# Tile 2's heads in tile 3's order, and its causal mask added once by VectorE to the decay columns

## What is computed

```python
def forgetting_attention(q, k, v, log_f):
    c = jnp.cumsum(log_f, axis=-1)
    for i in range(S // Q_BLOCK):                 # tiles of 128 queries
        q0, q1 = i * Q_BLOCK, (i + 1) * Q_BLOCK
        logits = jnp.einsum('bhqd,bhkd->bhqk', qf[:, :, q0:q1], kf[:, :, :q1])
        logits = logits + c[:, :, q0:q1, None] - c[:, :, None, :q1]
        logits = jnp.where(s_pos <= t_pos, logits, -jnp.inf)
        p = jax.nn.softmax(logits, axis=-1)
        outs.append(jnp.einsum('bhqk,bhkd->bhqd', p, vf[:, :, :q1]))
...
        mixed = jnp.concatenate([attn, pool], axis=-1)
        x = x + jnp.einsum('bse,ed->bsd', mixed, w_out[layer])
```

## Time and profile before

| | us |
|---|---|
| median of 3 runs | 2385.66 (2385.27 to 2389.16) |
| span of the profiled execution | 2541.9 |
| TensorE matmuls busy in it | 2151.2 (85%) |
| VectorE busy | 1499.3 (59%) |
| GpSimd busy | 1020.5 (40%) |
| ScalarE busy | 653.7 (26%) |
| mean granted TensorE clock | 0.898 |
| HBM traffic, mean | 330 GB/s |

### The profile page before, as it was taken

The page is one execution under the profiler, slowest core; times in us unless marked ns, Lnnn a source line. Parts: engine busy times, 40 slices in busy tenths (PEclk is TensorE's granted clock), DMA queues, the critical chain, the costliest instruction groups (busy, mean ns, idle before and its releaser), DMA issues.

```text
span 2541.9 us, 29123 instructions
## 1 busy us (share of the span) xinstructions
PE 2151.2 (85%) x10694; PEld 1516.7 (60%) x10694; DVE 1499.3 (59%) x3505; ACT 653.7 (26%) x1838; POOL 1020.5 (40%) x1028
## 2 busy tenths in 40 slices
PE   8999998999999986996675366276879799999998
PEld 7999785666666975874431254221366555545695
DVE  3441179999999368647454677710067665886321
ACT  6772235566555121001010101110122000001220
POOL 0000014555665113435566554566544544772000
PEclk8999999999998997998886567578887899999999
DMA  6767568999999978999999888999978998998485
GB/s 237 245 231 240 215 254 298 404 397 393 390 377 337 378 274 320 398 356 380 363 394 361 308 335 320 366 343 364 409 307 323 411 348 313 412 412 355 157 316 173
DMA packets 196750, 839.81 MB, mean 330 GB/s; under 512 B 22000, under 2 KB 22384, under 8 KB 164864
## 3 DMA queue, kind: packets, MB, share of 16 engines
q0 software_dynamic: 147456, 536.94, 54.8%
q1 hardware_dynamic: 43808, 290.72, 30.6%
q10 hardware_dynamic: 5344, 10.29, 1.3%
HBM read 835.70 MB, written 2.16 MB: 330 GB/s over the span
## 4 chain that ended last, share of the span: by engine, by line
PE 60%; DVE 15%; issue 10%; ACT 6%; POOL 5%; another core or an unknown queue 3%; DMA 2%; ACTq 0%; DVEq 0%; SPq 0%
PE ps L1200 59%; DVE rows L2745 7%; POOL rows L1172 5%; DVE ps L2769 1%; DMA rows<-in_pv,eidxT 1%; DVE h L2769 1%; DVE arena L2297 1%; DMA wr<-in_wso 1%; ACT arena L1734 1%; ACT L1871 1%; ACT arena L1865 0%; DMA wr<-in_wgate 0%; ACT L1801 0%; DVE arena L2359 0%
## 5 line engine op out<-in xcount | busy, mean ns | idle before, releaser
L1172 POOL DMA_INDIRECT rows<-in_pu,eidx x512 | 485.3, 948 | 936.6 <-DVE dots L2745 368.7
L1200 PE MATMUL ps<-arena,wr 128*128 128x128 f32 (+4 forms) x3968 | 771.9, 354 | 26.0 <-DMA wr<-in_wso 9.2
L1200 PEld LDWEIGHTS ps<-arena,wr 128*128 128x128 f32 x3968 | 606.9, 195 | 168.6 <-issue 27.3
L2745 DVE CUSTOM_DVE_ANT_0 rows<-rows,ps 128x1024 f32<-128x1024 f32 x512 | 594.0, 1217 | 11.3 <-DMA rows<-in_pu,eidx 5.5
L1200 PE MATMUL ps<-hT,wr 128*128 128x128 f32 (+2 forms) x1600 | 369.7, 390 | 44.6 <-issue 41.3
L1172 POOL DMA_INDIRECT rows<-in_pv,eidx x256 | 289.2, 1130 | 207.0 <-DVE h L2769 101.4
L1200 PEld LDWEIGHTS ps<-hT,wr 128*128 128x128 f32 x1600 | 262.5, 199 | 148.7 <-issue 57.6
L1172 POOL DMA_INDIRECT rows<-in_pv,eidxT x256 | 245.7, 960 | 142.9 <-issue 68.6
L1200 PE MATMUL ps<-rows,wz 128*32 128x512 f32 x1024 | 180.7, 778 | 78.5 <-DMA rows<-in_pv,eidxT 57.1
L1200 PE MATMUL ps<-wr,arena 128*128 128x256 f32 (+2 forms) x704 | 180.7, 412 | 2.1 <-ACT arena L1943 2.1
L2769 DVE SCALAR_TENSOR_TENSOR h<-rows,wgt,h 128x1024 f32<-128x1024 f32 x132 | 169.0, 1280 | 5.7 <-DMA rows<-in_pv,eidx 4.8
(11 more groups left out here) (403 smaller groups left out, 2258.3 us busy)
## 6 DMA issues: line engine op xcount, KB each, us to landing
wr<-in_wg SPq DMA_DIRECT2D x48, 1024.0 KB
wr<-in_wgu SPq DMA_DIRECT2D x33, 1024.0 KB
wr<-in_wgate SPq DMA_DIRECT2D x24, 1024.0 KB
wr<-in_wso SPq DMA_DIRECT2D x24, 1024.0 KB
wr<-in_wq SPq DMA_DIRECT2D x16, 1152.0 KB
wr<-in_wsc SPq DMA_DIRECT2D x16, 1024.0 KB
wr<-in_wqku SPq DMA_DIRECT2D x15, 1024.0 KB
wr<-in_wdn SPq DMA_DIRECT2D x14, 1024.0 KB
```

Source lines behind the costliest of these rows:

```text
L1172: e.indirect_dma_start(ring[slot_of[i]], None, A[table], bass.IndirectOffsetOnAxis(ap=index[:, t, k:k + 1], axis=0)).then_inc(gathered[slo ...
L1200: return e.matmul(o, l, r, start=start, stop=stop, skip_group_check=True)
L2745: e.tensor_tensor_reduce(row, row, wide[:], 1.0, 0.0, MUL, ADD, dots[:, k:k + 1]).then_inc(*dve.up(*u))
```

## The change

`MASKED` = 2 takes the place of the last tile's number in the places that deal with the mask: tile 2 now gets its mask as tile 3 does, by one addition to its columns of `cb` on VectorE. Since tile 3's attention needs tile 2's columns without the mask, ScalarE keeps a plain copy of them in `wz` (idle by then) and writes it back in the feed forward ("unmask"). "early" becomes true for tile 2: its second value product goes behind the second front, its pooled output products behind u_ = 4 and 8, the first of them in bank 4, the second in one of the ring. So the transposes of tile 2's odd heads from head 3 on use bank 5 like the even ones.

```diff
--- before.py
+++ after.py
@@ -37,6 +37,7 @@
 GROUPS = ((0, 1), (1, 2), (2, 4))
 SECOND = (("attend", 0, 2), ("attend", 2, 3), ("feed", 0, 3), ("attend", 3, 4), ("feed", 3, 4), ("out", 3, 4))
 VPE = (1, 2)
+MASKED = 2
 VW = 1.5
 SX = 1.8
 PLACES = ("early", "ring", "ring")
@@ -564,7 +565,7 @@
         if nt > 1 or j:
             pooled(j if nt > 1 else j - 1)
             yield True
-    early = t1 == NT and nt == 1
+    early = nt == 1
     for part in range(1 if early else 2):
         for t in range(nt):
             value(part, t)
@@ -577,8 +578,8 @@
         if t == 0:
             pl.load(("wout", t0, hf, part), A["wout2"][hf, part], 2048, ("pe", "wout", t0, hf, part, nt - 1))
         if part == 1:
-            if early:
-                pl.hold(("wout", t0, hf, t), 6 + hf, ("dve", "wout", t0, hf, t))
+            if early and (t1 == NT or hf == 0):
+                pl.hold(("wout", t0, hf, t), 6 + hf if t1 == NT else 4, ("dve", "wout", t0, hf, t))
             else:
                 pl.take(("wout", t0, hf, t), "lo", ("dve", "wout", t0, hf, t))
         pl.add("wout", t0, hf, part, t, p=mmc(512, 4), v=0.0 if part else vc(512))
@@ -593,9 +594,10 @@
                 kn = 128 * (t + 1)
                 if part == "front":
                     pl.take(("front", t, h), "lo", ("dve", "front", t, h))
-                    pl.add("front", t, h, p=(kn + 128 * (t0 < NT - 1)) / 600.0, v=vc(kn) + 2 * vc(1))
+                    pl.add("front", t, h, p=(kn + 128 * (t0 < MASKED)) / 600.0, v=vc(kn) + 2 * vc(1))
                 elif part == "texp":
-                    pl.hold(("texp", t, h), 4 - t % 2 if deep > 2 and h % 2 else 5, ("act", "texp", t, h))
+                    pl.hold(("texp", t, h), 4 - t % 2 if deep > 2 and h % 2 and (t1 == NT or h < 3) else 5,
+                            ("act", "texp", t, h))
                     pl.add("texp", t, h, p=0.12 * (t + 1))
                 else:
                     if h == 0:
@@ -608,8 +610,8 @@
         if early and u_ == 1:
             value(1, 0)
             yield True
-        if early and u_ in (4, 6):
-            wout((u_ - 4) // 2, 1, 0)
+        if early and u_ in ((4, 6) if t1 == NT else (4, 8)):
+            wout(int(u_ > 4), 1, 0)
             yield True
     pl.stage = ("wout", t0)
     for hf in range(2):
@@ -673,6 +675,8 @@
                 pl.add("fT", t0, j_, v=vc(nr))
                 yield True
         if j == 3:
+            if t0 < MASKED:
+                pl.add("unmask", MASKED)
             for a, b in outs:
                 yield from plan_out(pl, A, a, b)
         if j == 9:
@@ -883,6 +887,7 @@
         wT = sb("wT", [128, 128])
         xf = sb("xf", [128, 128])
         wz = [sb(f"wz{i}", [128, 16 * 32 + 32]) for i in range(2)]
+        plain_keys = [x[:, 0:512].rearrange("p (h k) -> p h k", h=4) for x in wz]
         dots = sb("dots", [128, 128])
         wgt = sb("wgt", [128, 128])
         st = sb("st", [128, G, 256])
@@ -1578,8 +1583,8 @@
                     b = ps(*u)
                     w.wait_ge(*(dve if ("at", t0) in PLAIN else act).at("qk", t0, 3, 1))
                     x = mm(b[:, 0:kn], AT[t0]["qT"][hp:hp + 64, h // 2, 128 * (t - t0):128 * (t - t0) + 128],
-                           kT[hp:hp + 64, h // 2, 0:kn], True, t0 == NT - 1)
-                    if t0 < NT - 1:
+                           kT[hp:hp + 64, h // 2, 0:kn], True, t0 >= MASKED)
+                    if t0 < MASKED:
                         x = mm(b[:, kn - 128:kn], ident, neg, False, True)
                     x.then_inc(*pe.up(*u))
 
@@ -1999,8 +2004,20 @@
                     nr = AT[t0]["hT"].shape[2]
                     b = bank[pl.bank["cb2", t0, h][0]]
                     w.wait_ge(*pe.at("cb2", t0, h))
+                    if t0 == MASKED:
+                        w.wait_ge(*pe.at("rows", MASKED, 31))
+                        e.activation(plain_keys[h // 4][:, h % 4, :], b[:, 0:nr], ACT.Copy
+                                     ).then_inc(*act.up("keys kept"))
                     e.activation(cb[:, h, 128 * t0:128 * t0 + nr], b[:, 0:nr], ACT.Copy
                                  ).then_inc(*act.up("cb2", t0, h))
+
+                elif kind == "unmask":
+                    t = u[1]
+                    w.wait_ge(*dve.at("front", t, 7))
+                    w.wait_ge(*act.at("keys kept"))
+                    for z in range(2):
+                        e.activation(cb[:, 4 * z:4 * z + 4, 128 * t:128 * t + 128], plain_keys[z], ACT.Copy
+                                     ).then_inc(*act.up("unmasked"))
 
                 elif kind == "front":
                     _, t, h = u
@@ -2564,7 +2581,7 @@
                     then()
                     e.tensor_tensor(up[:, 16:16 + nr], av[:, 16:16 + nr], up[:, 16:16 + nr], SUB
                                     ).then_inc(*dve.up("pooled", t0, j))
-                    if j == 3 and t0 == NT - 1:
+                    if j == 3 and t0 >= MASKED:
                         own_keys = cb[:, :, 128 * t0:128 * t0 + 128]
                         w.wait_ge(*act.at("cb2", t0, 7))
                         e.tensor_tensor(own_keys, own_keys, bmid(neg, 8), ADD).then_inc(*dve.up("masked", t0))
@@ -2624,6 +2641,8 @@
                     b = bank[pl.bank["front", t, h][0]]
                     w.wait_ge(*pe.at("front", t, h))
                     if t0 == NT - 1:
+                        w.wait_ge(*act.at("unmasked"))
+                    if t0 >= MASKED:
                         w.wait_ge(*dve.at("masked", t0))
                     else:
                         w.wait_ge(*act.at("cb2", t0, 7))
```

## The result

The change makes the kernel slower, by 0.3%. After: 2390.75 us median (2385.16 to 2398.87, 19 runs); before, timed beside it: 2384.96 us (2375.14 to 2389.16, 19 runs). The ratio is 1.003, with a 95% interval of 1.002 to 1.0041. The profiled execution of the changed kernel has a span of 2390.4 us, which fits its timed runs.

What follows compares the result with a forecast made beforehand. TensorE was taken to bound the kernel, so gains near tile 2 reach the end: 4.3 us from an earlier feed forward turn less 2.2 of lost clock, 2.1 off 2385.66, giving 2383.6 us; range 2375 to 2395.

Steps and rivals of the forecast that it cites:

- gain 4.7 us: End of tile 2's heads: the output's transposes start at 1936.8 instead of 1941.49, 4.7 us earlier.
- my 1.7 and 0.88: Tile 2's heads: TensorE waits of 1.7 us among the new heads, and 0.88 us for VectorE's division before the output's transposes.
- costs nothing: Tile 2's mask: VectorE's one addition of 1.22 us is covered by TensorE's work; without that cover, 1.2 us.
- a rule weighed: Tile 2's heads: if busy work releases the throttle, only the mask gains, 8 x 0.42 = 3.4 us, giving 2382.3 us.
- Ten dots fill less than 20 of 27 us: room.: VectorE in tile 2's heads: ten dots and eight softmax steps take less than 20 of its 27 us.
- What is late next: Behind tile 2's heads: VectorE's fifteen dots set the feed forward turn, at A + 25.4 against A + 25.0; gain 4.3 us.
- A: Start of the output's transposes behind tile 2's heads, the time from which the forecast counted to the feed forward turn.
- clock lost behind it: Behind tile 2's feed forward turn: the 9.8 us idle stretch costs TensorE clock, 0 to 3 us, taken as 2.2.
- 1, the clock falls in the new heads: Tile 2's heads: clock still falls, 2397.5 us, chance 0.16; for one stretch of 7 us only, 2387 us, chance 0.10.
- 2 and 4, the stalls under full DMA: Feed forward stalls: 2, they shrink, 2377.1 us, chance 0.22; 4, they move and grow, 2389 us, chance 0.08.
- 3, the end hangs on the gathers: Last tile's start: dots and value rows set it, not TensorE; 4.3 to 5 us gained, 2381 us, chance 0.12.

Runs made afterwards that it cites:

- mask fill: The mask only kernel plus unread identity products in two of TensorE's waits in tile 2's heads: 2377.5 us, ratio 0.9978 to the kernel before.
- order only: The changed kernel with the mask left on TensorE, so only the order of tile 2's products is new: ratio 1.0046 to the kernel before.
- after fill: The changed kernel plus unread identity products in three TensorE waits, two in tile 2's heads and one before its feed forward turn: 2386.68 us, ratio 1.0022.
- mask only: The changed kernel with the old order of tile 2's products, so only the mask's move to VectorE is new: ratio 1.0011 to the kernel before.
- before fill: The kernel before plus unread identity products in two of TensorE's waits in tile 2's heads: 2377.76 us, ratio 0.9981.
- the two draws: Two more traced runs of the unchanged kernel before: the first took 2377.45 us, the second, longer one 2386.29 us.

## Why the prediction was wrong

I forecast 2383.6 us, 2.1 below the median; it came out some 6 above, inside the range and on the other side.

**What bounds.** Right: TensorE, and what it loses near tile 2 arrives. The reading of the heads was wrong as a reading of the kernel. I wrote that TensorE has a clock of 0.50 in the heads of tile 2, which is more than even that one execution did: the stretch of the earlier trace rows leaves out the first four fronts, and in the earlier trace rows the logits at 1912.51 take 0.91 us, full speed. Over all of its heads that trace has 0.63. In the other trace of before in which the clock fell, five fronts came ahead of the fall; in two of the four traces of before it doesn't fall at all.

**The step that failed: "gain 4.7 us".** It took the heads of one low-clock execution for what the kernel does, and set against them new heads that were too short. Counted from tile 2's first turn to the output's transposes, I had 83.8 us now (1941.49 - 1857.69) and 79.1 then. Measured, before has 68.9 or 76.2, after 77.6 and 76.0 (its two traces): in place of a gain of 4.7 us, a loss of 7 to 9 against the shorter kind, and between 1.4 lost and 0.2 gained against the longer. Of the 83.8 us, 53.56 lay ahead of the first front, where ordinary executions have 47.2; that drops out of the difference. What doesn't is the heads. My base had 30.24 us for them against 21.70 or 28.98, my forecast 28.1 against 32.68 and 31.14. The step before it failed too, where I took differences from an execution 156 us too long at face value: I wrote that some of its idle time belonged to the profiling, and didn't ask whether its clock did.

Two parts of the forecast of the new heads I can check singly. The first front starts earlier by 2.3 us, against 2.5 (3.6 less one dot). A head is 1.93 or 2.24 us, against 1.84. In the one trace of the changed kernel with the clock held, the heads take 30.04 us; so some 2 us of my miss are not the clock (1.0 of them is idle time, 3.61 us in the changed kernel's trace in place of my 1.7 and 0.88), and 1.1 to 2.6 are.

**The mask, "costs nothing".** Not contradicted for VectorE and ScalarE (1.0011, 0.9993 to 1.003). I gave the removed products 3.4 us at full clock under "a rule weighed"; in the old order they are worth 0.5 to 0.7 (21.21 us for mask fill's heads, 21.70 or 21.92 with the products), in the new one at most 2.0 (32.08 in order only, 30.04 in after fill). What I missed is that they were work inside waits: without them the wait before the first product with the values grew from 1.22 to 1.76 us, and the only trace of mask only runs at half clock behind it.

**"Ten dots fill less than 20 of 27 us: room."** Right as a number and left unused: it says that VectorE would idle at the end of the heads (7.12 us), with the dots still to come.

**What is late next.** The best part of the sum: turn at A + 25.4 forecast, A + 25.35 and A + 27.0 measured; idle time 9.8 forecast, 9.94 measured; clock lost behind it 2.2 forecast, 2.8 to 3.2 measured. But "it is A + 25.0 now" was again the half-clock base: 24.64 with the clock low, 22.63 with it high. There the two additions had dots ahead of them at no cost, so this step alone loses 2.7 us.

With my own numbers for the changed kernel and the new traces as the base, the sum would have read so. A minus is time gained. Against the longer kind: first front -2.5, heads 28.1 - 28.98 = -0.9, transposes to turn 25.4 - 24.64 = +0.8, clock +2.2; together -0.4 us. Against the shorter kind: -2.5, 28.1 - 21.70 = +6.4, 25.4 - 22.63 = +2.8, +2.2; together +8.9 us. Between them lies a loss of some 4 us, where 5.8 was measured. The sign hung on the base.

**The rule weighed.** In the earlier trace rows, 22.32 of 23.20 us busy stood beside 0.50, and I went against the Trainium skill's "TensorE: Matmul & The Clock Gate", Part 1, by which sustained busy work releases the throttle. The runs split it. For holding a full clock they agree with it, as far as one trace can: with TensorE's waits filled (21.05 of 21.92 us busy) the clock stayed at 1.00. For getting it back, they don't; the narrow products of the heads did not do it here:

```profile
1799.54:1809.54 10.00, 10.00 (x37) 7.61 (x36) 5.45 (x17) 2.64 (x7) 1.88 (x2) 0.50 0.95 366
```

This is before, 2384.5 us: busy throughout and at the lower level; it comes back in the wide products, 15.50 us for four in place of 13.90. By the rule the heads would be at full speed already, and in two of the three ordinary traces of before they are; in the third they aren't, so neither reading holds for every execution, and one execution was too little to choose by. The time that I gave for the rule, 2382.3 us, is no nearer to the 2390.75 measured.

**The rivals.** 1, the clock falls in the new heads: true for one stretch, the case I gave 2387 us and 0.10; against before fill (2377.8), the clock is 4 to 6 of the 13 us. 2 and 4, the stalls under full DMA: they don't exist in executions of ordinary length. They stood 13 to 57 us behind the turn; in the 2375.7 us trace of before, whose turn is at 1831.40, TensorE works through that place with DMA just as full:

```profile
1839.90:1989.90 150.00, 150.00 (x510) 91.39 (x509) 105.35 (x171) 10.71 (x19) 77.86 (x83) 1.00 1.02 412
```

3, the end hangs on the gathers: no, or by very little. The wait for VectorE at the last tile's turn is between nothing and 1.9 us in every ordinary trace, and that is all the slack TensorE has there. The case that I hadn't written down is the one that came: VectorE's dots lose the output products that had hidden them.

**Left open.** Why the same program with the same wait of 1.22 or 1.23 us keeps its clock in one execution and loses it in the next. The 1.6 us that the changed kernel's first trace loses behind the last tile's turn (206.57 and 204.93) are no effect of the change: they are one product of 5.44 us in place of 3.81, absent from its second trace (204.95) and present in a trace of before (the first of the two draws, 2375.6 us).

## What to carry to other kernels

Wide products that are moved into a stretch fill it only if the waits there are theirs to fill; and they uncover whatever another engine was doing beside them, so ask first for whom they were the cover. Before a sum is built on a trace, its span is to be held against the timed runs, and a clock that it shows in one stretch is to be seen in a second trace. Where TensorE runs narrow products with waits of a microsecond between them, unread products in the waits are cheap to try: 14 of 128x64 went with a scatter of 7 us in place of 19 and a median lower by 0.2%, in twelve executions on one chip.

## What the runs showed of the chip

The granted clock is not a property of the program: one kernel has its eight heads at 1.00 in one execution and at 0.50 from the sixth front on in another, 9 us apart in span (2375.7 and 2384.5), and the same kernel with two of its waits filled had twelve executions between 2375 and 2382 us. The mean clock of a whole execution doesn't tell the two apart: mask fill's trace has 0.926 with its heads at 1.00, the longer draw of before 0.929 with 0.66. A clock that has fallen stayed at 0.50 through 10 us of unbroken narrow products and rose in 128x512 ones. A wait of 1.22 us ahead of the same transposes is followed by full clock in order only, and one of 1.07 us by half clock in the changed kernel, so the length of the wait alone doesn't decide. Removing TensorE work may cost TensorE time: with eight mask products gone, the one trace has heads of 28.05 us, where before has 21.70 or 28.98; that it is more than the fall which before shows too is suggested by the twelve times, not shown.
